# Bank reads moved to VectorE with one semaphore per PSUM bank, spread rotary angles, and the next norm's input rounded from scaled x, on one Trainium2 core

## The reference, cut to what matters

```python
r   = 1 / sqrt(mean(x*x, over the 1024 features) + eps)      # one number per position
out = (x * r * gain) @ w
x   = x + mixer(out)
```

## Time and profile before

| | |
|---|---|
| median of three runs | 3581.18 us |
| the profiled execution, and its span | 3586.0 us, 3584.2 us |
| TensorE matmuls busy | 3280.0 us, 92% |
| VectorE busy | 1544.6 us, 43% |
| ScalarE busy | 766.5 us, 21% |
| GpSimd busy | 1999.2 us, 56% |
| mean granted TensorE clock | 0.94 of full |

### The profile page before, as it was taken

The page is one execution under the profiler, slowest core; times in us unless marked ns, Lnnn a source line. Parts: engine busy times, 40 slices in busy tenths (PEclk is TensorE's granted clock), DMA queues, the critical chain, the costliest instruction groups (busy, mean ns, idle before and its releaser), DMA issues.

```text
span 3584.2 us, 45625 instructions
## 1 busy us (share of the span) xinstructions
PE 3280.0 (92%) x14188; PEld 2550.8 (71%) x14188; DVE 1544.6 (43%) x2422; ACT 766.5 (21%) x1562; POOL 1999.2 (56%) x1528
## 2 busy tenths in 40 slices
PE   4898999999888899998898878989999999989998
PEld 3564887888666378787786656868887676868886
DVE  5545226221555453443325545662225454662223
ACT  3421102000244111110102334230002233231001
POOL 4234666776642276675666131847767332747775
PEclk8897999999989899999999789999999999999999
DMA  4111223222221122222222010313232111312322
GB/s 145 36 42 60 94 95 105 96 98 95 93 77 36 37 98 96 91 94 83 93 88 84 24 62 24 109 59 100 94 100 94 48 54 36 101 65 94 100 94 88
DMA packets 78350, 285.00 MB, mean 80 GB/s; under 512 B 8688, under 2 KB 9200, under 8 KB 77424
## 3 DMA queue, kind: packets, MB, share of 16 engines
q1 hardware_dynamic: 74736, 269.41, 22.7%
q10 hardware_dynamic: 3456, 13.50, 1.0%
HBM read 280.78 MB, written 2.10 MB: 79 GB/s over the span
## 4 chain that ended last, share of the span: by engine, by line
PE 76%; DVE 16%; ACT 3%; issue 3%; DVEq 1%; DMA 1%; ACTq 0%; SPq 0%
PE pa L493 35%; PE pd L493 31%; PE pd L635 3%; PE po L654 3%; DVE qs L167 2%; DVE h_lo L167 1%; DVE work L167 1%; DVE pair L167 1%; DVE b_lo L167 1%; PE po L687 1%; PE pa L643 1%; PE pd L673 1%; DVE work L171 1%; ACT work L163 1%; ACT pair L163 1%
## 5 line engine op out<-in xcount | busy, mean ns | idle before, releaser
L446 POOL TENSOR_SCALAR w_hi<-w_raw 128x1024 fp32r<-128x1024 f32 x508 | 554.6, 1092 | 1513.1 <-PE pa L493 964.1
L493 PE MATMUL pa<-h_hi,w_hi 128*128 128x512 f32 x1888 | 763.8, 405 | 55.4 <-issue 25.4
L450 POOL TENSOR_TENSOR w_lo<-w_raw,w_hi 128x512 fp32r<-128x512 f32 x508 | 750.5, 1477 | 0.0
L493 PE MATMUL pa<-h_lo,w_hi 128*128 128x512 f32 x1888 | 747.9, 396 | 0.0
L493 PE MATMUL pa<-h_hi,w_lo 128*128 128x512 f32 x1888 | 746.6, 395 | 0.0
L448 POOL TENSOR_TENSOR w_lo<-w_raw,w_hi 128x512 fp32r<-128x512 f32 x508 | 716.7, 1411 | 42.3
L493 PE MATMUL pd<-b_hi,w_hi 128*128 128x512 f32 x1152 | 460.8, 400 | 60.0 <-DVE x_res L167 39.4
L493 PEld LDWEIGHTS pa<-h_hi,w_hi 128*128 128x128 f32 x1888 | 362.5, 192 | 164.5 <-issue 72.9
L493 PE MATMUL pd<-b_hi,w_lo 128*128 128x512 f32 x1152 | 454.1, 394 | 0.0
L493 PE MATMUL pd<-b_lo,w_hi 128*128 128x512 f32 x1152 | 454.1, 394 | 0.0
L493 PEld LDWEIGHTS pa<-h_hi,w_lo 128*128 128x128 f32 x1888 | 362.3, 192 | 78.1
(11 more groups left out here) (154 smaller groups left out, 3642.8 us busy)
## 6 DMA issues: line engine op xcount, KB each, us to landing
w_raw<-in_w SPq DMA_DIRECT2D x508, 512.0 KB, 3.2
mrg<-in_mem ACTq DMA_DIRECT2D x4, 1024.0 KB, 4.8
mrg<-in_nabias ACTq DMA_DIRECT2D x2, 2048.0 KB, 8.4
x_res<-in_x SPq DMA_DIRECT2D x8, 256.0 KB, 6.0
out_y<-mrg ACTq DMA_DIRECT2D x8, 256.0 KB, 2.1
mrg<-in_count ACTq DMA_DIRECT2D x2, 512.0 KB, 3.6
kbuf<-in_delta ACTq DMA_DIRECT2D x2, 448.0 KB, 8.1
rope<-in_rope SPq DMA_DIRECT2D x1, 512.0 KB, 12.2
```

What stands on the lines that cost most here:

```text
L446: nc.gpsimd.tensor_scalar(w_hi[:, j], raw[:, j % RR], 1.0, 1.0, ALU.mult, ALU.mult).then_inc(rounded, 1)
L450: nc.gpsimd.tensor_tensor(w_lo[:, j, 512:1024], raw[:, j % RR, 512:1024], w_hi[:, j, 512:1024].bitcast(F32), ALU.subtract).then_inc(wsplit, 1)
L493: ins = mm(out, a, b, start=(first and k == 0 and e == 0), stop=(last and k == k_n - 1 and e == 2))
```

## The change

Four things change, and some bookkeeping with them.

1. `pa_done` becomes four semaphores, one per bank, so that two engines may read banks in any order; `wait_read(eng, n, i)` waits for the reading of the i-th. TensorE waits for the four banks of the cross queries one by one, the gates' VectorE likewise.
2. Where ScalarE copied a bank and VectorE scaled the copy, VectorE now reads the bank and writes the scaled result (`rooted`), and frees the bank. At O, ScalarE rounds `b_hi` straight from `po`, and VectorE subtracts it from `po`.
3. `prepare`: ScalarE rounds `h_hi` from `x * gain` in one instruction, then squares; VectorE forms `h_lo = x * gain - h_hi` in one instruction, then adds the squares up in the PSUM bank `po[0]`; the eighth sum goes to `acc` in SBUF. The residual loops with a preparation are unrolled on VectorE and ScalarE.
4. `angles` becomes a generator; in groups 0 and 1 of that block three of its steps follow each `up`, and those two loops are unrolled on VectorE.

```diff
@@ TensorE
             def bank_a():
                 i = n.take("pa_done")
-                pe.wait_ge(pa_done, n.free("pa_done", i, RA))
+                wait_read(pe, n, i - RA)
@@ ScalarE
-            def prepare(m, split=True):
+            def prepare(m, name=None):
                 i = n.take("acc_part")
                 act.wait_ge(x_full, n.last("x_full"))
+                if name:
+                    hi(h_hi[:, m], x[:, m], col(name, m))
                 act.wait_ge(acc_part, n.free("acc_part", i, 2))
-                f(pair2[:, i % 2], tile_of(x, m), ACT.Square).then_inc(sx_full, 1)
-                if split:
-                    hi_t(tile_of(h_hi, m))
+                f(pair2[:, i % 2], x[:, m], ACT.Square).then_inc(sx_full, 1)
...
                 elif what == "Cv":
-                    dst = turned(ph.kind, p)
...
-                        take_a(dst)
-                    n.take("late")
+                    not_here()
...
                     elif what == "O":
-                        n.take("pv_done")
+                        o = n.take("pv_done")
                         if a == tiles - 1:
-                            hi_t(b_hi[:, ph.out + p])
+                            act.wait_ge(pv_done, n.at("pv_done", o))
...
+                                hi(b_hi[:, ph.out + p], po[p % 2][:, :])
@@ VectorE
             def clear_sum():
-                if n.n.get("acc_used"):
-                    dve.wait_ge(acc_used, n.last("acc_used"))
-                chain(v.memset(acc, 0.0))
+                chain(v.memset(po[0][:, :], 0.0))
 
             def prepare(m, name, split=True):
                 if split:
-                    tt = n.take("t_full")
...
-                    v.tensor_scalar(t[:, tt % 2], xtile(m), gain, None, ALU.mult).then_inc(t_full, 1)
+                    g = n.take("split_full")
+                    dve.wait_ge(hi_full, n.at("hi_full", g))
+                    v.scalar_tensor_tensor(h_lo[:, m], x[:, m], col(name, m), h_hi[:, m].bitcast(F32), ALU.mult,
+                                           ALU.subtract).then_inc(split_full, 1)
                 i = n.take("acc_part")
                 dve.wait_ge(sx_full, n.at("sx_full", i))
-                v.tensor_tensor(acc, acc, pair2[:, i % 2], ALU.add).then_inc(acc_part, 1)
-                if split:
-                    lo(dst, t[:, tt % 2], high)
+                if m == KT - 1 and n.n.get("acc_used"):
+                    dve.wait_ge(acc_used, n.last("acc_used"))
+                v.tensor_tensor(acc if m == KT - 1 else po[0][:, :], po[0][:, :], pair2[:, i % 2], ALU.add)\
+                    .then_inc(acc_part, 1)
...
-            def late_scale(buf, grouped=False):
-                dve.wait_ge(pa_done, n.last("pa_done"))
-                n.take("late")
-                root = rx[:, :]
+            def rooted(dst, grouped=False, scale=None):
+                n.take("cdone")
+                dve.wait_ge(cdone, n.last("cdone"))
+                i = n.take("pa_done")
+                src, root = pa[i % RA][:, :], rx[:, :]
...
-                v.tensor_tensor(buf, buf, root, ALU.mult).then_inc(late, 1)
+                    ins = v.tensor_tensor(dst, src, root, ALU.mult)
...
+                ins.release(pa_done, i)
...
                     elif what == "O":
                         o = n.take("pv_done")
                         if a == len(ph.tiles) - 1:
-                            dve.wait_ge(pv_done, n.at("pv_done", o))
+                            mine, high, low = po[p % 2][:, :], b_hi[:, ph.out + p], b_lo[:, ph.out + p]
...
-                                g = to_t(lambda q: v.tensor_copy(q, po[p % 2][:, :]))
-                            lo_t(ph.out + p, g)
+                            lo(low, mine, high)
...
-                    if g == 8:
+                    if beside and number < 2:
+                        steps = beside(number)
+                        for j in range(g):
+                            up(j)
+                            for _ in range(3):
+                                next(steps, None)
+                        assert next(steps, "none") == "none"
+                    elif g == 8:
```

More of the change, by code:

```diff
@@ L102, in last, with bank @@
         return self.at(name, self.n.get(name, 0) - 1)
+    def bank(self, i):
+        return i % RA, i // RA + 2 + self.loop.get("banks", 0)
     def free(self, name, i, ring):
@@ L116, in repeat @@
                 self.loop[name] = old.get(name, 0) + i * k
+            self.loop["banks"] = old.get("banks", 0) + i * (per.get("pa_done", 0) // RA)
+            assert per.get("pa_done", 0) % RA == 0
             yield i
@@ L156, in wait @@
     def wait(self):
-        if self.last:
+        if self.last and self.item is not None:
+            self.eng.wait_ge(self.last, self.counts.bank(self.item)[1])
+        elif self.last:
             c, name = self.counts, self.last.name
@@ L411, in build, with wait_read @@
         block = ctx.enter_context(nc.Block())
+        def wait_read(eng, n, i):
+            b, count = n.bank(i)
+            eng.wait_ge(pa_done[b], count)
         def col(name, k=0):
@@ L569, in piece @@
                         note_qs()
-                    if ph.kind in ("na", "mem", "cross"):
-                        n.take("late")
+                    else:
+                        n.cross_item = n.n["pa_done"] - 1
                 elif what == "Cv":
                     linear(bank_a()).then_inc(cdone, 1)
-                    n.vt_item = n.take("late")
+                    n.vt_item = n.n["pa_done"] - 1
                 elif what == "M":
@@ L594, in piece @@
                     linear(bank_a()).then_inc(cdone, 1)
-                    n.take("late")
+                    if what == "Cg":
+                        n.take("late")
                 elif what == "Cm":
@@ L625, in attend @@
                             if ph.kind == "cross":
-                                pe.wait_ge(late, n.last("late"))
+                                for back in range(3, -1, -1):
+                                    wait_read(pe, n, n.cross_item - back)
                         bank = bank_d()
@@ L1065, in piece @@
                 elif what in LATENTS.pieces():
-                    take_a(crope[:, LATENTS.pieces().index(what)])
-                    n.take("late")
+                    n.latent = not_here()
                 elif what == "Cm":
@@ L1155, in pool_mix, with residual @@
                 for m in range(2):
-                    take_a(mrg[:, 2 * m:2 * m + 2].rearrange("p a n -> p (a n)")[:, 16:16 + S])
+                    not_here()
                 for m in range(2):
                     hi_t(b_hi[:, 2 + m])
-            def residual(prep=False, split=True):
-                if not prep:
+            def residual(sums=False, name=None):
+                if not sums:
                     n.n["cdone"] += 8
@@ L1165, in residual, with ffn @@
                     return
-                per = {"cdone": 4, "x_full": 4, "acc_part": 4}
-                if split:
-                    per.update(t_full=4, split_full=4)
-                with n.repeat(act, 2, per) as r:
-                    for m in range(4):
-                        n.take("cdone")
-                        n.take("x_full")
-                        prepare(r * 4 + m, split)
-            def ffn(last=False, between=None):
+                for m in range(KT):
+                    n.take("cdone")
+                    n.take("x_full")
+                    prepare(m, name)
+            def ffn(next_name=None, between=None):
                 stream_norm()
@@ L1194, in ffn @@
                         log_and_exp()
-                    residual(ends, not last)
+                    residual(ends, next_name)
             def gates():
@@ L1306, in _ @@
             i, q = to_qs()
-            act.wait_ge(late, n.last("late"))
+            for back in range(4, -1, -1):
+                wait_read(act, n, n.latent - back)
             for m in range(3):
@@ L1323, in _ @@
             n.n["cdone"] += 3
-            residual(True)
+            residual(True, "b0_x")
             def cross_and_ffn(l):
@@ L1339, in _ @@
             load_mem("mem2")
-            residual(True)
+            residual(True, "b1_x")
             cross_and_ffn(1)
@@ L1525, in piece @@
                 elif what in LATENTS.pieces():
-                    n.take("cdone")
-                    note_a()
-                    late_scale(crope[:, LATENTS.pieces().index(what)])
+                    rooted(crope[:, LATENTS.pieces().index(what)])
                 elif what == "Cg":
@@ L1650, in pool_mix @@
                 for m in range(2):
-                    n.take("cdone")
-                    note_a()
-                    dve.wait_ge(pa_done, n.last("pa_done"))
-                    chain(v.tensor_tensor(flat(m, 0, S), flat(m, 0, S), rx[:, :], ALU.mult))
+                    rooted(flat(m, 0, S))
+                    wait_read(dve, n, n.n["pa_done"] - 1)
```

(7 more changed lines are left out.)

173 lines of the change are left out of this document (81 added, 92 removed).

## The result

| | before | changed |
|---|---|---|
| median | 3581.69 us (4 runs, 3576.22 to 3583.19) | 3447.05 us (4 runs, 3441.26 to 3452.21) |
| ratio, 95% interval | | 0.9626 [0.9607, 0.9646] |
| profiled execution, span | 3586.0, 3584.2 us | 3441.26, 3439.4 us |
| mean granted clock | 0.94 | 0.96 |

The profiled execution of the changed kernel is the fastest of its four, so the same kernel was profiled a second time (`changed_again`: 3449.21 us, span 3447.4).

A forecast was written before the change was run, and what follows sets the result against it. TensorE, busy 92% of the span, was taken as the bound, with its waits for VectorE. Angles 24.5, residual ends 42, start 5.6 and attention 20.9 sum to 93.0 us: 3586.0 becomes 3493.0 profiled, 3488 as median; range 3465 to 3530.

The forecast's parts named there:

- all four places: Where VectorE is late for TensorE: angles, ends of residuals with a norm behind, start, attention; 93.0 us together.
- 3509: Rival: the hops saved in attention are followed by another wait, so attention gives nothing; 3509 us, chance 0.16.
- 3526: Rival: residual ends stay VectorE's through a 1.50 us PSUM write or longer added hop; 3526 us, chance 0.10.
- 3500: Rival: angle steps spread among the ups stall them, giving half the angle gain back; 3500 us, chance 0.05.
- the windows behind the angles: TensorE's two waits behind the angle operations, with slow matmuls after, go by spreading the steps: 24.5 us.
- 3590: Rival: 46 banks wait in VectorE's queue, making the kernel slower; 3590 us at 2.2 us each, chance 0.02.
- Nine such places ...: 9.4: Scaling from the bank, eight in dilated attention and one in sliding window: each removes a 1.04 us wait, 9.4 us.
- For the other 21 ... I take 0.35: Ends of pairs outside mla and dil: 0.35 us each, between 0 and 1.38, together 7.4 us.
- The eight of dil are covered by TensorE's products: Ends of pairs in dilated attention: hidden behind TensorE's products, so no gain was counted.
- The cross outputs: Two cross output projections: VectorE stays the bound, a tile takes 3.97 instead of 4.22 us; 5 each, 10 us.
- The low end: Bottom of the range, all upper bounds but a few: 24.5 + 52 + 8 + 32 = 116 us gained, 3465 us.
- the 37 other scalings: Scalings from the bank outside the nine places: taken at nothing, since head roots, pooling chain or other products follow.

The follow-up runs named there:

- the kernel with three memsets: Changed kernel with three dummy memsets on VectorE between its wait for the values' bank and its read, at the dilated stage's eight pairs: 3478.8 us.

## Why the prediction was wrong

**Sign and main mechanism were right.** VectorE's lateness in front of TensorE is what went, at all four places, and none of the rivals came: 3509 needed attention to give nothing, 3526 a slow write to PSUM (it took 0.70), 3500 stalled ups (the windows behind the angles gave 24.9 of 24.5), 3590 held banks. What should show, showed: `x_res` 3.0, "issue" of 5 us gone at the feed-forward ends, a tile 4.10, the first product at 37.34, 46 reads fewer.

**The step that failed: "Nine such places ...: 9.4".** It priced a wait of 1.04 us at 1.04 us. Undone, it cost the dilated stage 20.3 us for seven waits, since TensorE runs at half clock behind most of them. The clock was in the prediction, but only behind waits of 5 and 10 us, where the chain showed 7.40 for 4.76. The same view of a stretch behind a short wait would have shown it. So would the stage's granted clock: 0.94 over the 258 us from 2787 to 3045 is some 31 us at half clock, 15 us of time. That row I had read before the forecast, and left it out of the sum. The term is 12 us short (8.4 of it stood for that stage).

**"For the other 21 ... I take 0.35".** The end of a pair gave 19.2 and not 11.5. By stage the three of mla gave 4.9 where 4.1 was forecast, and the 21 others 10.9 where 7.4 was: 3.6 in sliding window, 7.3 in the cross stages and the second cross output. "The eight of dil are covered by TensorE's products" held but for 1.2 us of idle time; the rest of that stage's 4.4 is half clock at its head, which came and went without this edit.

**The cross outputs: 18.0 and not 10.** I carried the slow `h_lo` of 1.38 over from a feed-forward end. There GpSimd is busy 37.07 us of 41.22; in b0's cross output it is busy 19.80 of 31.89, and `h_lo` took 0.75 to 0.78 in five of the seven tiles that follow the first, and 1.57 in one. The tile became 3.25 where I had 3.97, "issue" fell from 4.96 to 1.88 where I left 3, and b1's 10.2 us of half clock went altogether.

**The bounds were too narrow on that side.** Attention had 35 as its upper bound, all of it waiting time, and gave 52.2 by the second profile. The low end took 52 and 32 in place of the stated bounds 57 and 35, but those, 124.5 in sum and 3457 us, would have missed too. With 52 in place of 32 the low end's sum, 24.5 + 52 + 8 + 52, is 136.5, and 3445 would have held the result. An upper bound made of lengths of waits isn't one.

**What stays open.** Of the 26.4 us in the other attention stages, the kernels with one part undone put 13.2 on the ends of pairs and about 4 on the 37 other scalings; 9 are not assigned, and single profiles of those stages scatter by 5. Whether a wait between 0.73 and 1.04 us costs clock wasn't tried, nor whether other matmuls around it would change that.

## What to carry to other kernels

Price a wait of TensorE by what the granted clock does behind it, not by its length: in this one stage a wait of 0.73 us cost little more than itself, one of 1.04 cost 2.4 and one of 1.96 cost 4.3. Before forecasting, read the granted clock of each stage that the change touches, and count up to half of its time at half clock, where TensorE has work, as within reach of an edit that takes the waits away: in the dilated stage all of it went, in the other attention 28.0 us of 263.1. And when a filler is put into a kernel to measure a wait, look first whether the engine was idle there.

## What the runs showed of the hardware

- Short idle times of TensorE bring it from 2.4 to 1.2 GHz even where it is busy 93% of a stage: 34.1 us at half clock behind 13.7 us of waits, in the kernel with three memsets.
- Two executions of one kernel with the same waits can differ in half clock: 64.9 and 78.5 us in one stage, with 35.8 and 35.7 us idle.
- A VectorE operation on 128x512 with one operand in PSUM and one in SBUF takes the same time everywhere, also when it writes the bank that it reads: 77 sums at 700 ns in the mean, 173 scalings at 692. With both inputs in SBUF a multiplication or subtraction of the same size takes 0.69 to 1.6, and `h_lo`, which multiplies and subtracts, 0.75 to 1.87. Where the start was followed, in the rotations above, it was GpSimd's own two-input operation that set the end. The three groups of the changed kernel (count, busy us, mean ns, idle before):

```profile
L180 DVE TENSOR_TENSOR work<-pa,rx 128x512 f32<-128x512 f32 x173 | 119.7, 692 | 441.6 <-PE pa L512 437.9 <-DVE rx L188 0.9
L188 DVE SCALAR_TENSOR_TENSOR h_lo<-x_res,par,h_hi 128x512 fp32r<-128x512 f32 x80 | 106.9, 1336 | 62.5 <-ACT h_hi L176 61.5
...
L180 DVE TENSOR_TENSOR po<-po,pair 128x512 f32<-128x512 f32 x77 | 53.9, 700 | 12.9 <-ACT pair L176 5.3 <-DVE h_lo L188 0.5
```

The Trainium skill, "SBUF — State Buffer", section "Who interferes with whom", says that a VectorE instruction with two SBUF inputs contends with GpSimd's reads and one with at most one SBUF input does not. The rows agree: 692 and 700 ns against 1336.
